# Expert gathers for 64 tokens and two ranks in place of 32 tokens and four, with the routing spread out to match

## The chip, the cores and the metric

One core of a Trainium2 chip runs the kernel, in one launch. The metric is the time of one execution in microseconds (us), measured on the device; lower is better. All arithmetic is in fp32.

## The reference, cut to what matters

One inference step of a one-layer trunk, for 1024 prompt tokens and 32 sample tokens. The change touches the last part, a retrieval feed-forward: every token has eight heads, every head picks 16 of 16384 experts, and an expert is one row of `u` and one row of `v`.

```python
def block_tail(x, o_sb, o_sw, ...):
    h = x + merged @ w_out
    return h + peer_ffn(rms_norm(h, g_ffn), w_q, keys_1, keys_2, u, v)

def peer_ffn(x, w_q, keys_1, keys_2, u, v):
    q = (xt @ w_q).reshape(t, 8, 2, 128)
    s1, s2 = q[:, :, 0] . keys_1, q[:, :, 1] . keys_2      # (t, 8, 128) each
    v1, i1 = top_k(s1, 16);  v2, i2 = top_k(s2, 16)
    best, pos = top_k(v1[..., :, None] + v2[..., None, :], 16)
    idx, gate = experts of pos, softmax(best)
    hid = gelu(einsum('thkd,td->thk', u[idx], x))
    y = einsum('thk,thkd->td', gate * hid, v[idx])
```

Ahead of it come a combined projection, stick-breaking attention over all earlier tokens, window attention with ALiBi, and the output projection. A final RMSNorm follows.

## The kernel before

**Two phases.** A projection phase (to about 350 us of the span) writes all q, k and v to scratch. The fused phase then does everything else, with every engine's program unrolled over the same line of *slots*, numbered n. Each engine walks the slots in order and issues, in a fixed order within a slot, whatever the tables `STEP_AT`, `WINDOW_AT`, `TAIL_AT`, `ROUTE_AT`, `GROUP_AT`, `X_AT` and `FINISH_AT` place there. Engines meet only through semaphores, so one that is late holds up whoever waits for it, and everything behind that wait on the waiting engine.

**The gathers.** A slot n from 0 to 1055 has one gather of 1 MB: an indirect DMA by GpSimd (L683) fetches, into each of 128 partitions, the 8 KB row `[u, v]` of one expert. Partition p belongs to one of 32 tokens and to one of four ranks (`COPIES` is 4). A group is 32 tokens and 32 gathers; a tile of 128 tokens is four groups, 128 gathers. There are eight tiles and a ninth of the 32 sample tokens: 33 groups. The ring `uv` holds seven gathers (`RING`), so gather n is issued when the expert matmuls of gather n-7 are done (`vmm`). For each gather, VectorE multiplies the u half by the tokens' x and sums (L891); for each pair of gathers (a batch) ScalarE takes gelu (L824) and makes two diagonal matrices (L830) of `gate * hid`, 128x32 each; TensorE then multiplies them with the v halves into `y_acc` (L1338). Of a batch, one gather writes one column group of 32 and the other its neighbour; the next batch writes the other two. GpSimd prepares the gates on the diagonal once in four gathers (`spread_gates`, L667).

**Once in a group.** ScalarE copies `y_acc` out (`group_out`, L840), and the first batch of the next group waits for that copy; TensorE folds the four copies together (L1326), VectorE adds (L1082). TensorE also writes x for the coming group to `o_sw` in 32 small matmuls (`copies_of_x`, L1272), and ScalarE copies it to `x_rep` in two halves (`copy_x`, L801).

**Routing.** For every head of every tile, `ROUTE_AT` places eleven stages: queries (TensorE, L1286) at offset 0, key scores at 3, seven stages of top-k on VectorE at offsets 4 to 9 and 11 (`first_eight` to `spread`), and a `select` at 10 (L1317) that brings the chosen indices into the layout of the gathers. Heads start nine slots apart, from slot 128t - 54 of tile t, and four slots apart for the first tile.

**What is placed around it.** All of it is relative to the first head's slot of a tile. `tail_slot` is 23 slots before it: merging, output projection in four quarters (L1250, slots +9 to +12), the residual on VectorE (L985, +14), its square on ScalarE (L774, +15), the turned xn (L1260, +19). `window_slot` is another 20 before that, with window attention's maximum (L934) on VectorE one slot later; it waits for a DMA of distances and window values issued two slots before. The stick-breaking steps, one in four slots, end right before the window; tile t has 2(t+1) of them, the sample tile 17.

In the running tile (positions 0 to 127 of its own slots) this places the next tile's steps up to position 29, its window at 31 to 49, its tail at 51 to 72, and its routing from 74 to position 20 of the next tile. Groups end at positions 0, 32, 64 and 96.

```python
def route_slot(t, head):
    return 4 * head - 22 if t == 0 else t * P - 54 + 9 * head
GROUP_AT = {(g + 1) * TS: g for g in range(GATHERS // TS)}
X_AT = {TS * (g - 1) + 2 * b if g else 2 * b - 18: (g, b) for g in range(GATHERS // TS) for b in range(2)}
```

## Time and profile before

| | |
|---|---|
| time, median of 3 runs | 3571.81 us (3557.09 to 3578.2) |
| time of the profiled execution | 3575.88 us |
| its span | 3574.2 us |
| VectorE busy | 63% |
| TensorE matmuls busy | 74% |
| indirect gathers | 1056, 1 MB each |
| first gather issued at | 462.83 us |

The span runs from the first to the last instruction. The shares are averages over the whole span; the fused phase has to be read by stretches. The fourth tile is cut below into eight stretches, which begin at its positions 0, 24, 40, 64, 74, 96, 104 and 112. Positions in time were found by the start of the VectorE product L891 of a given gather, which stands once per slot; the view that lists it counts two instructions for each (the product and the read of its sum).

### The profile page before, as it was taken

To read this page: it belongs to the slowest core of one execution; us is meant where nothing else is said; L and a number is where in the kernel's file an instruction comes from. 1 tells how busy PE (TensorE), PEld (TensorE's weight loads), DVE (VectorE), ACT (ScalarE), POOL (GpSimd) and SP (SyncE) were. 2 spreads that over 40 slices of the span, in tenths; PEclk is the share of its full clock that TensorE was granted. 3 is DMA by queue.
4 is the path that set the end of the run, shared out by engine and by line. 5 is a ranking of instruction groups with operands and counts; after the bars stand their busy time and mean duration, and the time that the engine had idled before them with its cause. 6 is when DMAs were issued, how large, how long until landed. Compare 5 with 4: busy or idle time off the path is not lost.

```text
span 3574.2 us, 44480 instructions
## 1 busy us (share of the span) xinstructions
PE 2648.0 (74%) x13804; PEld 1181.2 (33%) x13804; DVE 2235.2 (63%) x5671; ACT 1407.2 (39%) x3271; POOL 1434.9 (40%) x1363
## 2 busy tenths in 40 slices
PE   7998667676767777777768867887688767757675
PEld 4544342222323332333223322332244223422221
DVE  2110175578657855786568756875688557655786
ACT  1000224333632453345435633564266424443332
POOL 0000014455445534554454445444444444334543
PEclk9999687888888988898888988988999888878887
DMA  5221249999999999999899999999999999998997
GB/s 226 90 84 68 83 162 359 389 408 399 374 386 409 400 344 380 410 390 360 363 401 391 379 372 383 391 368 375 387 375 378 350 383 368 348 347 364 393 399 312
DMA packets 249016, 1210.63 MB, mean 339 GB/s; under 512 B 28944, under 2 KB 98352, under 8 KB 112592
## 3 DMA queue, kind: packets, MB, share of 16 engines
q0 software_dynamic: 156416, 1122.51, 78.8%
q1 hardware_dynamic: 92368, 85.34, 7.4%
q8 instruction: 108, 1.77, 0.2%
q14 instruction: 124, 1.02, 0.1%
HBM read 1183.96 MB, written 28.38 MB: 339 GB/s over the span
## 4 chain that ended last, share of the span: by engine, by line
PE 33%; DMA 22%; DVE 11%; issue 7%; ACTq 6%; ACT 6%; POOL 2%; DVEq 2%; SPq 0%; POOLq 0%
DMA f_uv<-peer_uv,f_idx 19%; PE f_y_acc L1338 15%; DVE f_uv L891 5%; PE f_q_ps L1286 4%; PE f_z L1250 4%; ACTq L828 3%; DMA f_work<-cache_sb_kT 3%; ACTq L716 3%; PE f_z L1143 2%; POOL f_uv L683 2%; PE f_z L1162 2%; ACT f_diag L830 2%; PE f_z L1169 1%; ACT f_work L717 1%; DMA f_work<-scratch_projT 1%
## 5 line engine op out<-in xcount | busy, mean ns | idle before, releaser
L683 POOL DMA_INDIRECT f_uv<-peer_uv,f_idx x1056 | 1247.0, 1181 | 1655.6 <-PE f_y_acc L1338 1392.3
L1338 PE MATMUL f_y_acc<-f_uv,f_diag 128*32 128x512 f32 x4224 | 1230.3, 710 | 623.1 <-ACT f_diag L830 540.2
L891 DVE CUSTOM_DVE_ANT_0 f_uv<-f_uv,f_x_rep 128x1024 f32<-128x1024 f32 x1056 | 1294.4, 1231 | 590.8 <-DMA f_uv<-peer_uv,f_idx 583.8
L1338 PEld LDWEIGHTS f_y_acc<-f_uv,f_diag 128*32 128x32 f32 x4224 | 228.0, 120 | 1279.9 <-ACT f_diag L830 719.5
L824 ACT ACTIVATE f_act_hid<-f_hid 128x2 f32<-128x2 f32 x528 | 106.8, 202 | 1070.6 <-DVE f_hid L891 1068.7
L1286 PE MATMUL f_q_ps<-w_q,f_xnT 128*128 128x256 f32 x1152 | 297.4, 416 | 28.5 <-DVE f_cut L1010 25.2
L830 ACT ACTIVATE f_diag<-f_gate_fold,f_act_hid 128x32 f32<-128x32 f32 x1056 | 282.2, 314 | 38.7 <-issue 2.8
L283 PE MATMUL proj<-xnT,w_cols 128*128 128x512 f32 (+1 forms) x864 | 283.9, 491 | 2.1 <-DVE nat L251 1.6
L1286 PEld LDWEIGHTS f_q_ps<-w_q,f_xnT 128*128 128x128 f32 x1152 | 237.2, 211 | 129.1 <-issue 56.2
L824 ACT ACT_TABLE_LOAD x207 | 265.6, 1283 | 3.8
L698 ACT ACT_TABLE_LOAD x120 | 154.0, 1283 | 254.4 <-PE f_z L1169 226.2
L667 POOL TENSOR_TENSOR f_gate_fold<-f_fold,f_gates 128x128 f32<-128x128 f32 x264 | 162.4, 615 | 125.6 <-DVE f_gates L1075 120.5
L283 PEld LDWEIGHTS proj<-xnT,w_cols 128*128 128x128 f32 x864 | 143.6, 193 | 142.8 <-issue 142.2
L241 DVE TENSOR_SCALAR stage<-proj 128x512 f32<-128x512 f32 x18 | 12.4, 692 | 270.7 <-PE proj L283 270.7
L1250 PE MATMUL f_z<-w_out_sb,f_work 128*128 128x512 f32 (+1 forms) x288 | 146.5, 664 | 25.7 <-DVE f_work L978 25.7
L304 POOL DMA_DIRECT2D scratch_projT<-stage x18 | 10.0, 555 | 311.8 <-DVE stage L241 311.8
L206 ACT ACTIVATE stage<-proj 128x512 f32<-128x512 f32 x18 | 10.8, 599 | 293.2 <-PE proj L283 293.2
L1186 PEld LDWEIGHTS f_o_sb<-f_work 128*128 128x128 f32 (+2 forms) x848 | 88.8, 169 | 55.2 <-ACT f_work L730 48.9
L1143 PE MATMUL f_z<-f_q_pad,f_work 128*128 128x256 f32 x288 | 104.9, 499 | 1.6 <-DMA f_work<-scratch_projT 1.6
L1186 PE MATMUL f_o_sb<-f_work 128*128 128x64 f32 (+2 forms) x848 | 97.8, 263 | 8.1 <-DMA f_work<-cache_sb_v 3.3
L1162 PE MATMUL f_z<-f_work,f_neg_suffix 128*128 128x512 f32 (+2 forms) x178 | 99.5, 644 | 5.3 <-DVE f_work L919 4.3
L913 DVE SCALAR_TENSOR_TENSOR f_work<-f_z,f_work 128x512 f32<-128x512 f32 (+2 forms) x89 | 56.9, 640 | 65.4 <-ACT f_work L719 61.3
(152 smaller groups left out, 2802.7 us busy)
## 6 DMA issues: line engine op xcount, KB each, us to landing
f_uv<-peer_uv,f_idx POOLq DMA_INDIRECT x1056, 9.5
f_work<-scratch_projT SPq DMA_DIRECT2D x86, 128.0 KB, 8.9
scratch_projT<-stage POOLq DMA_DIRECT2D x18, 528.0 KB, 3.9
w_cols<-w_in SPq DMA_DIRECT2D x18, 512.0 KB, 3.8
f_work<-scratch_nat SPq DMA_DIRECT2D x72, 128.0 KB
w_q<-w_peer_q SPq DMA_DIRECT2D x1, 8192.0 KB, 24.9
scratch_nat<-nat POOLq DMA_DIRECT2D x10, 512.0 KB, 3.4
x_in<-x_prompt SPq DMA_DIRECT2D x8, 512.0 KB, 4.1
```

What stands on the lines that cost most here:

```text
L283: last = nc.tensor.matmul(acc[s][:, a:b], w[:, s, k, :], xnT[:, k, a:b], start=(k == 0), stop=(k == DK - 1))
L667: nc.gpsimd.tensor_tensor(gate_fold[:, tick % 4, :, :], fold[:].unsqueeze(1).broadcast_to(full), gates[:, t % 2, head, j * PART:(j + 1) * ...
L683: pool.indirect_dma_start(uv[:, n % RING, :], None, io["peer_uv"], bass.IndirectOffsetOnAxis(ap=idx[:, t % 2, head, k:k + 1], axis=0),).th ...
L824: nc.scalar.activation(act_hid[:, tick % 2, first:first + 2], hid[:, tick % 4, first:first + 2], ACT.Gelu)
L830: made = nc.scalar.activation(diag[:, tick % 2, i, :], gate_fold[:, tick % 4, i, :], ACT.Copy, scale=act_hid[:, tick % 2, i:i + 1])
L891: nc.vector.tensor_tensor_reduce(row_u, row_u, x_rep[:, g % 2, :], 1.0, 0.0, ALU.mult, ALU.add, hid[:, tick % 4, n % PART:n % PART + 1]).t ...
L1143: last = nc.tensor.matmul(z[:, at:at + 256], kT[:, (e % 2) * 256 + m * P:(e % 2) * 256 + (m + 1) * P], q_pad[:, f, m, :, :].rearrange("p a ...
L1162: nc.tensor.matmul(out, neg_suffix[0:keys, 0:keys], sp[0:keys, 0:width], start=False, stop=False, skip_group_check=True)
L1186: last = nc.tensor.matmul(o_sb[0:n, hd * HD:(hd + 1) * HD], probs[0:keys, i * n:(i + 1) * n], v_blk[0:keys, col:col + HD], start=(e == 0 a ...
L1250: last = nc.tensor.matmul(z[0:rows, b * 512:(b + 1) * 512], mergedT[:, k, 0:rows], w_out[:, k, b * 512:(b + 1) * 512], start=(k == 0), sto ...
L1286: last = nc.tensor.matmul(q_ps[:, 0:2 * QH], xnT[:, k, :], w_q[:, k, head * 2 * QH:(head + 1) * 2 * QH], start=(k == 0), stop=(k == DK - 1))
L1338: last = nc.tensor.matmul(y_acc[i * TS:(i + 1) * TS, b * 512:(b + 1) * 512], diag[:, tick % 2, i, :], uv[:, n % RING, DM + b * 512:DM + (b ...
```

## The change

A gather now serves 64 tokens and two ranks. A group is 64 tokens and 64 gathers, so there are 17 groups, the last one of the 32 sample tokens. The diagonal matrices are 128x64, and a batch's two gathers write the two column groups of 64. `copies_of_x` has 16 matmuls where it had 32, `select` 4 where it had 16. `spread_gates` is issued after every second gather, for two ranks of 64 tokens, where it was issued before every fourth for four ranks of 32; both write 128x128. The diagonal buffer holds three batches in place of four. Routing starts 16 slots earlier in a tile and its heads are 15 slots apart (12 in the second tile, 11 in the sample tile, 8 in the first). The window, the tail and the steps, which are placed relative to it, move 16 slots earlier with it (8 slots later in the second tile). Positions in the running tile, for the third tile on: steps to 13, window 15 to 33, tail 35 to 56, routing 58 to position 46 of the next tile, groups' ends at 0 and 64.

```diff
 RING = 7
-COPIES = P // TS
+GT = 64
+COPIES = P // GT
 PART = TOPK // COPIES
+SAMPLE_COPIES = P // TS
...
-    return 4 * head - 22 if t == 0 else t * P - 54 + 9 * head
+    if t == 0:
+        return 8 * head - 22
+    return 82 + 12 * head if t == 1 else t * P - 70 + (15 if t < NT else 11) * head
...
+NG = 2 * NT + 1
...
-GROUP_AT = {(g + 1) * TS: g for g in range(GATHERS // TS)}
-X_AT = {TS * (g - 1) + 2 * b if g else 2 * b - 18: (g, b) for g in range(GATHERS // TS) for b in range(2)}
+GROUP_AT = {min((g + 1) * GT, GATHERS): g for g in range(NG)}
+X_AT = {GT * (g - 1) + 40 * (g % 2 == 0) + 2 * b if g else 2 * b - 18: (g, b) for g in range(NG) for b in range(2)}
...
-        hid = sb("hid", [P, 4, PART])
-        act_hid = sb("act_hid", [P, 2, PART])
-        gate_fold = sb("gate_fold", [P, 4, PART, TS])
-        diag = sb("diag", [P, 2, PART, TS])
+        hid = sb("hid", [P, 8, 2])
+        act_hid = sb("act_hid", [P, 4, 2])
+        gate_fold = sb("gate_fold", [P, 4, 2, GT])
+        diag = sb("diag", [P, 3, 2, GT])
...
-            hold(pool, S["routed"], 1)
-            spread_gates(0)
             for n in range(GATHERS):
                 g, t, j, head, rank = expert_of(n)
                 if rank == 0:
                     hold(pool, S["routed"], t * PH + head + 1)
-                if rank == 3 and n + 1 < GATHERS:
-                    hold(pool, S["routed"], routed_by(n // 4 + 1))
-                    spread_gates(n // 4 + 1)
                 if n >= RING:
                     hold(pool, S["vmm"], n - RING + 1)
                 k = j * PART + rank
                 pool.indirect_dma_start(uv[:, n % RING, :], None, io["peer_uv"],
                                         bass.IndirectOffsetOnAxis(ap=idx[:, t % 2, head, k:k + 1], axis=0),
                                         ).then_inc(S_UV[n % RING], 16)
+                if n % 2 == 0:
+                    spread_gates(n // 2)
...
                 for k in range(4 * b, 4 * b + 4):
                     for c in range(COPIES):
-                        last = nc.tensor.matmul(o_sw[c * TS:(c + 1) * TS, k % 4 * P:(k % 4 + 1) * P],
-                                                xnT[:, k, g % 4 * TS:(g % 4 + 1) * TS], ident[:], start=True, stop=True,
+                        last = nc.tensor.matmul(o_sw[c * GT:(c + 1) * GT, k % 4 * P:(k % 4 + 1) * P],
+                                                xnT[:, k, g % 2 * GT:(g % 2 + 1) * GT], ident[:], start=True, stop=True,
                                                 skip_group_check=True)
...
             def experts(batch):
-                tick, first = batch // 2, batch % 2 * 2
-                opens = tick % PH == 0
+                opens = 2 * batch % GT == 0
                 pe.wait_ge(S["diag"], batch + 1)
-                if opens and tick:
-                    pe.wait_ge(S["y_ev"], tick // PH)
+                if opens and batch:
+                    pe.wait_ge(S["y_ev"], 2 * batch // GT)
                 for b in range(2):
-                    for i in range(first, first + 2):
-                        n = tick * PART + i
-                        last = nc.tensor.matmul(y_acc[i * TS:(i + 1) * TS, b * 512:(b + 1) * 512], diag[:, tick % 2, i, :],
+                    for i in range(2):
+                        n = 2 * batch + i
+                        last = nc.tensor.matmul(y_acc[i * GT:(i + 1) * GT, b * 512:(b + 1) * 512], diag[:, batch % 3, i, :],
                                                 uv[:, n % RING, DM + b * 512:DM + (b + 1) * 512],
                                                 start=opens, stop=False, skip_group_check=True)
```

## Rows read from the trace of the kernel before

**Rows 1.** The page: span, busy time by engine, DMA in 40 slices.

```profile
span 3574.2 us, 44480 instructions
...
PE 2648.0 (74%) x13804; PEld 1181.2 (33%) x13804; DVE 2235.2 (63%) x5671; ACT 1407.2 (39%) x3271; POOL 1434.9 (40%) x1363
...
GB/s 226 90 84 68 83 162 359 389 408 399 374 386 409 400 344 380 410 390 360 363 401 391 379 372 383 391 368 375 387 375 378 350 383 368 348 347 364 393 399 312
```

**Rows 2.** The page's costliest groups, those of the gather and its work.

```profile
L683 POOL DMA_INDIRECT f_uv<-peer_uv,f_idx x1056 | 1247.0, 1181 | 1655.6 <-PE f_y_acc L1338 1392.3
L891 DVE CUSTOM_DVE_ANT_0 f_uv<-f_uv,f_x_rep 128x1024 f32<-128x1024 f32 x1056 | 1294.4, 1231 | 590.8 <-DMA f_uv<-peer_uv,f_idx 583.8
L667 POOL TENSOR_TENSOR f_gate_fold<-f_fold,f_gates 128x128 f32<-128x128 f32 x264 | 162.4, 615 | 125.6 <-DVE f_gates L1075 120.5
```

**Rows 3.** Stretches, L891 alone: the first 32 slots, then two whole tiles.

```profile
core 0: us, DVE busy (x), PEclk, DMA share, GB/s
494.13:601.61 107.48, 39.10 (x64) 0.77 0.73 275
...
1585.52:1957.62 372.10, 157.83 (x256) 0.86 0.96 378
...
2704.82:3099.53 394.71, 157.64 (x256) 0.86 0.94 364
```

**Rows 4.** The fourth tile in eight stretches, all engines; lengths are in the second column.

```profile
core 0: us, PE busy (x) PEld busy (x) DVE busy (x) ACT busy (x) POOL busy (x), PEclk, DMA share, GB/s
1585.52:1658.88 73.36, 62.48 (x374) 29.52 (x364) 58.11 (x151) 48.42 (x92) 31.27 (x30) 0.88 0.98 370
1658.88:1715.46 56.58, 39.94 (x204) 16.68 (x203) 26.41 (x53) 29.52 (x62) 20.21 (x22) 0.82 0.85 319
1715.46:1776.73 61.27, 41.89 (x149) 14.65 (x150) 36.94 (x73) 23.05 (x66) 28.95 (x29) 0.86 1.00 410
1776.73:1811.15 34.42, 26.58 (x154) 12.26 (x153) 16.50 (x29) 11.64 (x32) 12.88 (x13) 0.85 0.93 348
1811.15:1870.27 59.12, 41.38 (x239) 15.64 (x239) 43.85 (x120) 16.35 (x48) 33.43 (x30) 0.83 1.00 406
1870.27:1890.39 20.12, 13.78 (x116) 6.30 (x112) 18.89 (x55) 6.98 (x17) 8.08 (x8) 0.92 0.99 387
1890.39:1911.77 21.38, 16.16 (x79) 7.18 (x81) 18.98 (x54) 10.79 (x23) 10.24 (x10) 0.84 1.00 401
1911.77:1957.62 45.85, 39.51 (x210) 17.95 (x202) 40.53 (x114) 23.66 (x51) 21.52 (x20) 0.89 0.99 393
```

**Rows 5.** Who waited for whom: window attention's maximum. In total, times, longest.

```profile
DVE f_work L934 <- issue: 48.5, 7, 9.9
```

**Rows 6.** Timeline of ScalarE and VectorE at the third tile's position 65: start, length, instruction, idle.

```profile
1416.59 1.23 DVE L985 TENSOR_TENSOR f_work<-f_z,f_work 128x1024 f32<-128x1024 f32 x1 [4.44 <-PE f_z L1250]
...
1417.63 0.60 ACT L801 ACTIVATE f_x_rep<-f_o_sw 128x512 f32<-128x512 f32 x1 [11.31 <-PE f_o_sw L1272]
```

**Rows 7.** Timeline at the first gathers, GpSimd and VectorE.

```profile
462.83 1.04 POOL L683 DMA_INDIRECT f_uv<-peer_uv,f_idx  x1 [0.44 <-issue]
...
494.13 1.21 DVE L891 CUSTOM_DVE_ANT_0 f_uv<-f_uv,f_x_rep 128x1024 f32<-128x1024 f32 x1
```

**Rows 8.** Groups by line: ScalarE's diagonal and a copy of 128 columns.

```profile
L830 ACT ACTIVATE f_diag<-f_gate_fold,f_act_hid 128x32 f32<-128x32 f32 x1056 | 282.2, 314 | 38.7 <-issue 2.8
...
L794 ACT ACTIVATE f_xnT<-f_z,f_g_ffn 128x128 f32<-128x128 f32 x72 | 19.4, 376 | 3.8 <-PE f_z L1260 3.8
```

**Rows 9.** TensorE's timeline: two batches in a row, then full-width products.

```profile
700.57 1.91 PE L1338 MATMUL f_y_acc<-f_uv,f_diag 128*32 128x512 f32 x8 [0.37 <-ACT f_y_part L840]
...
703.15 1.46 PE L1338 MATMUL f_y_acc<-f_uv,f_diag 128*32 128x512 f32 x6
...
571.39 1.16 PE L1162 MATMUL f_z<-f_work,f_neg_suffix 128*128 128x512 f32 x2
...
424.62 2.31 PE L1250 MATMUL f_z<-w_out_sb,f_work 128*128 128x512 f32 x5
```

More of the change, by code:

```diff
@@ L64, in constants @@
     c["dist_sample"] = np.abs(qs[:, None] - ks[None, :]).astype(np.float32)
-    c["fold"] = np.tile(np.eye(TS, dtype=np.float32), (P // TS, 1))
+    c["fold"] = np.tile(np.eye(GT, dtype=np.float32), (P // GT, 1))
     return c
@@ L377, in fused_phase @@
         hidden = sb("hidden", [P, P])
-        fold = sb("fold", [P, TS])
+        fold = sb("fold", [P, GT])
         iota = sb("iota", [P, 2, TOPK])
@@ L482, in expert_of @@
         def expert_of(n):
-            g, s = divmod(n, TS)
-            return (g, g // 4, g % 4, *divmod(s, PART))
+            g, s = divmod(n, GT)
+            return (g, g // 2, g % 2, *divmod(s, PART if g < NG - 1 else TOPK // SAMPLE_COPIES))
         @block.sync
@@ L655, in _, with spread_gates @@
             hold(pool, S["const"], 14 * 16)
[L657 to L668 removed]
+            def spread_gates(batch):
+                g, t, j, head, rank = expert_of(2 * batch)
+                hold(pool, S["routed"], t * PH + head + 1)
+                if batch >= 4:
+                    pool.wait_ge(S["diag"], batch - 3)
+                full = [P, 2, GT]
+                k = j * PART + rank
+                nc.gpsimd.tensor_tensor(gate_fold[:, batch % 4, :, :], fold[:].unsqueeze(1).broadcast_to(full),
+                                        gates[:, t % 2, head, k:k + 2].unsqueeze(2).broadcast_to(full),
                                         ALU.mult).then_inc(S["gate_fold"], 1)
[L671 to L672 removed]
             for n in range(GATHERS):
@@ L1314, in select @@
                 sel_free(n, r)
-                for j in range(4 if t < NT else 1):
-                    for c in range(COPIES):
-                        last = nc.tensor.matmul(sel_ps[c * TS:(c + 1) * TS, j * 8:(j + 1) * 8], ident[:, j * TS:(j + 1) * TS],
-                                                packed[:, c * PART:(c + 1) * PART, :].rearrange("p k two -> p (k two)"),
+                size, copies = (GT, COPIES) if t < NT else (TS, SAMPLE_COPIES)
+                ranks = TOPK // copies
+                for j in range(rows_of(t) // size):
+                    for c in range(copies):
+                        last = nc.tensor.matmul(sel_ps[c * size:(c + 1) * size, j * 2 * ranks:(j + 1) * 2 * ranks],
+                                                ident[:, j * size:(j + 1) * size],
+                                                packed[:, c * ranks:(c + 1) * ranks, :].rearrange("p k two -> p (k two)"),
                                                 start=True, stop=True, skip_group_check=True)
@@ L1324, in fold_group @@
                 sel_free(n, sum(slot + 10 <= n for slot in ROUTE_AT))
-                rows = slice(g % 4 * TS, (g % 4 + 1) * TS)
-                nc.tensor.matmul(sel_ps[rows, :], fold[:], y_part[:, b * 512:(b + 1) * 512], start=True, stop=True,
-                                 skip_group_check=True).then_inc(S["y_fold"], 1)
+                size = GT if g < NG - 1 else TS
+                rows = slice(g % 2 * GT, g % 2 * GT + size)
+                for f in range(0, GT, size):
+                    last = nc.tensor.matmul(sel_ps[rows, :], fold[:, f:f + size], y_part[:, b * 512:(b + 1) * 512],
+                                            start=(f == 0), stop=(f + size == GT), skip_group_check=True)
+                last.then_inc(S["y_fold"], 1)
             def experts(batch):
-                tick, first = batch // 2, batch % 2 * 2
-                opens = tick % PH == 0
+                opens = 2 * batch % GT == 0
                 pe.wait_ge(S["diag"], batch + 1)
-                if opens and tick:
-                    pe.wait_ge(S["y_ev"], tick // PH)
+                if opens and batch:
+                    pe.wait_ge(S["y_ev"], 2 * batch // GT)
                 for b in range(2):
-                    for i in range(first, first + 2):
-                        n = tick * PART + i
-                        last = nc.tensor.matmul(y_acc[i * TS:(i + 1) * TS, b * 512:(b + 1) * 512], diag[:, tick % 2, i, :],
+                    for i in range(2):
+                        n = 2 * batch + i
+                        last = nc.tensor.matmul(y_acc[i * GT:(i + 1) * GT, b * 512:(b + 1) * 512], diag[:, batch % 3, i, :],
                                                 uv[:, n % RING, DM + b * 512:DM + (b + 1) * 512],
```

56 lines of the change are left out of this document (22 added, 34 removed).

## The prediction

> **What bounds the kernel now.** I read the page first. Averages name no engine as the bound: TensorE's matmuls are busy for 74% of the span and VectorE for 63% [rows 1]. The data rate does: from the eighth of the 40 slices to the last but one it stays between 344 and 410 GB/s [rows 1]. The costliest groups say who waits. Each of the 1056 gathers waits for a free buffer, and GpSimd sits idle 1392.3 us for TensorE's L1338; VectorE in turn waits 583.8 us for gathered rows [rows 2]. So work runs round a loop of seven buffers. It goes at the speed of the DMA as long as landing, product, gelu, diagonal and matmul come round in time, and at the speed of the loop where they don't.
>
> The stretches tell the two apart. Position 40 to 64 of the fourth tile takes 61.27 us for 24 slots, 2.55 us each, at 410 GB/s and a DMA share of 1.00 [rows 4]. That is the floor, and this change moves the same bytes. Against 2.55 us a slot, the eight stretches of that tile stand at +12.2, +15.8, 0, +8.9, +3.0, -0.3, +1.0 and +5.1 us [rows 4]. Their sum is 46 us of the tile's 372.10 us; the seventh tile, with the sample's long attention beside it, takes 394.71 us [rows 3]. The first 32 slots take 107.48 us, 26 over the floor [rows 3], and 31.3 us pass between the first gather's issue and the first product (462.83 to 494.13) [rows 7]. Only such excess can be won back.
>
> **The start.** Between slots -11 and 0 VectorE now works at the routing of four heads at once, about 2.9 heads' worth of stages by the offsets, so 31.3 / 2.9 = 10.8 us a head. With eight slots between heads about 1.4 remain ahead of slot 0: 15 us, unless landing takes longer. The product of slot 0 comes 16 us earlier. The first seven gathers now need one head alone where they needed two. After it, two heads less are crowded into slots 0 to 16, which I value at half of the 26 us: 13. Sum -30 us (bounds: -15, if TensorE's queries take back the second part; -42, if both parts of the excess go).
>
> **Fewer group ends.** Each of them costs ScalarE a copy, TensorE the copies of x, and the batch that opens the next group a wait. What that is worth depends on the place. At position 96, in a quiet stretch, it is nothing: 20.12 us for eight slots, -0.3 over the floor [rows 4]; I take 0.5 us. At 32 the loop is already dry, because VectorE waits there for window attention's DMA (48.5 us in 7 times [rows 5], 6.9 us each); the copy and its handshake come on top of that, 1.5 us. At 64 the end meets the tail. ScalarE stands 11.31 us at `copy_x`, since TensorE has the output projection ahead of the copies of x; gelu and diagonals of the next batch are queued behind it [rows 6]. In the new table no copy of x and no group end lies in the tail (35 to 56). The projection stays, and VectorE's 4.44 us wait for it [rows 6] too, so only what the group end adds goes: two turns of x copies and the fold, about 3 us of the 8.9. Per tile 0.5 + 1.5 + 3 = 5; eight tiles, -40 us (bounds -8 and -72, at 1 and 9 us a tile). The work saved on ScalarE, TensorE and VectorE elsewhere lies beside the DMA and counts nothing.
>
> **Routing 15 slots apart.** Position 74 to 96 prices a head on VectorE: 43.85 us busy, less 22 products at 1.24 us (1.23 in [rows 2], and its read), leaves 16.6 us for two heads, 8.3 each [rows 4]. Position 0 to 24 has 58.11 - 29.8 = 28.3 us for some 2.1 heads and six steps, so a step is about 1.8 us. Heads nine slots apart beside steps need 9 x 1.24 + 8.3 + 2.25 x 1.8 = 23.5 us in 22.95: VectorE falls behind. Fifteen apart they need 33.7 us in 38.3. The excess of the routing stretches (12.2 + 5.1 beside steps, 3.0 without) I put down to routing by half of the first and all of the second: 11.7 us a tile. In the new table about 3.6 heads lie in quiet slots at 0.8, two beside steps at 0.7, and one falls into VectorE's wait for the window's DMA, which its work fills (-1.5). But the last two now overlap window and tail, where routing never was: +2 and +1.5. That leaves about 6.5; the gain is 5 us, and I take 4. Seven tiles: -28 us. No row shows routing beside the projection, so the bounds are +21 (3 us a tile lost) and -42.
>
> **Wider operands.** A diagonal takes ScalarE about 21 ns longer (from 314 ns at 32 columns and 376 at 128 [rows 8], a third of the difference), two of them 42, and the weights load somewhat slower; where the loop sets the pace that is a seventh of some 0.1 us a batch, 5 us in all. GpSimd runs 528 gate spreads for 264, at 615 ns [rows 2]: +162 us of its time, but issued right after an even gather, when it would wait for TensorE anyway (1655.6 us idle ahead of its gathers [rows 2]). Products beside a spread are slightly longer: 3 us. Together +8 us (bounds +3, +15). If GpSimd's cover is gone, 0.6 us falls on every second gather where the loop is the bound, some 70 us.
>
> **Do the wide column groups overlap?** All else hangs on this. A batch is eight instructions of 512 columns in 1.91 us; full-width ones take 1.16 us for two and 2.31 for five, 0.38 us for each more, so eight one after the other need 1.16 + 6 x 0.38 = 3.5 us [rows 9]. The batch's two gathers thus run side by side on two column groups. The next batch does not join them: two adjacent ones take from 700.57 to 703.15 + 1.46, 4.04 us [rows 9]. The new code has two groups of 64 in a batch; I expect 1.9 us again.
>
> The Trainium skill, in TensorEngine Tiling (Array Packing), Theoretical Speedup, gives four-fold packing for 32 columns and two-fold for 64, which speaks against the change. By that page a batch would lose up to half its rate; the row at 4.04 us shows that four-fold packing was never used here.
>
> **Sum.** 3575.9 (the profiled time, 1.7 us over its span and 4 over the median of the runs) - 30 - 40 - 28 + 8 = 3486 us; less the 4 us, 3482 us.
>
> **Rivals.**
> 1. *Routing against the tail* (chance 0.2). Head seven's queries and top-k come just ahead of the projection, head six beside the window. For it: TensorE is already busy 26.58 of 34.42 us from 64 to 74 [rows 4]. Against: the queries end some six slots before the projection. Only the start and a few group ends remain: 3572 - 30 - 8 + 8 = 3542 us, and up to 3563 with the +21.
> 2. *The loop stays as it is* (0.14). The excess comes from steps, window and projection by themselves, and group ends and routing ride beside them. For it: position 24 to 40 has the largest excess with VectorE busy only 26.41 of 56.58 us [rows 4]. Then half of the start is all: 3572 - 15 + 8 = 3565 us.
> 3. *Column groups of 64 don't overlap* (0.07), the case on the other side. A batch takes 3.5 us, +1.6 for each of 64 batches a tile: 102 us more on TensorE, 281 busy us of the fourth tile's 372 [rows 4] become 383. From 0 to 24 that is 62.5 + 19 = 82 for 73 us, from 112 on 39.5 + 13 = 52.5 for 45.9; with the tail about +25 us a tile: 3482 + 8 x 25 = 3682 us. It decides once a batch takes over about 2.4 us.
> 4. *A wait replaces the old one* (0.07). The last head of the second tile is ready seven slots before its gather, and GpSimd issues about four ahead; a routing that is late by more than three slots stops the gathers. At 5 us a tile, with no gain from routing: 3482 + 28 + 40 = 3550 us; from 10 us a tile (3590) it would be slower.
> 5. *More comes back* (0.12). All bounds on the good side: 3572 - 42 - 72 - 42 + 3 = 3419 us.
>
> **How the numbers follow.** The forecast has 0.4, around 3482 us, its own range 3445 to 3530. The upper rivals reach 3565, rival 5 reaches 3419; with rival 3 left out, 3430 to 3575 holds eight in ten. A measurement of this kernel tells about 0.5% (18 us) from no change. Faster: 0.4 + rival 5's 0.12 + 0.16 of rival 1 + 0.07 of rivals 2 and 4 = 0.75. Slower: rival 3's 0.07, and 0.06 from the far ends of rivals 1, 2 and 4. Same: the remaining 0.12.
>
> **What would show it.** L1338's batch of eight at 1.9 us, its PE time as before. First product near 478 us. About 360 us for the middle tiles in place of 372; no `copy_x` wait over 3 us; L934's wait nearer 4 than 7 us; the quiet stretches still at 2.55 us a slot. Wrong if batches take over 2.4 us, if GpSimd waits for `routed` (the gates' copy) in every tile, or if the quiet slot itself changes.

## The result, and the profile after

| | median of 10 runs | lowest to highest | profiled run | its span |
|---|---|---|---|---|
| before | 3560.22 us | 3554.12 to 3578.2 | 3575.88 us | 3574.2 us |
| after | 3589.2 us | 3580.72 to 3601.93 | 3601.93 us | 3600.3 us |

The changed kernel is slower: the ratio is 1.0077 (95% interval 1.0056 to 1.0097), some 27 us. The forecast was 3482 us, with 0.75 on faster. The page of the changed kernel, to be read against [rows 1] and [rows 2]:

```profile
span 3600.3 us, 38253 instructions
...
PE 2657.9 (74%) x10640; PEld 1211.6 (34%) x10640; DVE 2225.9 (62%) x5639; ACT 1388.4 (39%) x3211; POOL 1541.9 (43%) x1627
...
L680 POOL DMA_INDIRECT f_uv<-peer_uv,f_idx x1056 | 1210.2, 1146 | 1691.4 <-PE f_y_acc L1339 1368.2
L1339 PE MATMUL f_y_acc<-f_uv,f_diag 128*64 128x512 f32 x4224 | 1300.7, 740 | 585.3 <-ACT f_diag L828 547.3
L888 DVE CUSTOM_DVE_ANT_0 f_uv<-f_uv,f_x_rep 128x1024 f32<-128x1024 f32 x1056 | 1296.6, 1235 | 598.6 <-DMA f_uv<-peer_uv,f_idx 592.8
L828 ACT ACTIVATE f_diag<-f_gate_fold,f_act_hid 128x64 f32<-128x64 f32 x1056 | 310.1, 340 | 38.0 <-issue 2.0
L669 POOL TENSOR_TENSOR f_gate_fold<-f_fold,f_gates 128x128 f32<-128x128 f32 x528 | 306.2, 580 | 10.6
```

6227 instructions fewer, among them 3164 matmuls of TensorE and as many weight loads. GpSimd is 107 us busier with its spreads, weight loads 30 us; the other engines are within 20 us of before. The loop waits as it did: GpSimd 1368.2 us for TensorE, VectorE 592.8 us for gathered rows. So the averages don't tell where 26 us of span went; the stretches do. First the start, GpSimd's first gather and VectorE's first product (compare [rows 7]):

```profile
453.02 1.01 POOL L680 DMA_INDIRECT f_uv<-peer_uv,f_idx  x1 [99.26 <-DVE f_gates L1072]
...
466.23 1.21 DVE L888 CUSTOM_DVE_ANT_0 f_uv<-f_uv,f_x_rep 128x1024 f32<-128x1024 f32 x1
```

Then the gathered part by the product's instructions alone: slots 0 to 31, 32 to 255, 256 to 895 (the third to seventh tile), 896 to 1055. After:

```profile
core 0: us, DVE busy (x), PEclk, DMA share, GB/s
466.23:552.82 86.59, 39.19 (x64) 0.88 0.94 369
552.82:1196.41 643.59, 278.27 (x448) 0.85 0.96 380
1196.41:3129.23 1932.82, 787.38 (x1280) 0.85 0.94 367
3129.23:3579.37 450.14, 198.15 (x318) 0.81 0.94 376
```

And the kernel before, in the same stretches (its first one is in [rows 3]):

```profile
601.61:1218.18 616.57, 276.67 (x448) 0.88 0.98 394
1218.18:3099.53 1881.35, 789.06 (x1280) 0.87 0.96 376
3099.53:3555.99 456.46, 196.20 (x318) 0.82 0.95 377
```

Slot 32 starts at 552.8 us instead of 601.6, 48.8 us earlier: more than the 30 forecast. Slots 32 to 255 give 27.0 us back, the five middle tiles lose 51.5 us, 10.3 each, and the last stretch gains 6.3. With 2.7 us more behind the last product the sum is the 26.1 us by which the spans differ. A second profile of the changed kernel had 1945.6 us for the middle tiles, so a difference of some 13 us over them, 2.6 a tile, says nothing.

**Where in a tile.** The fourth tile of the changed kernel, its positions 32 to 56, 56 to 64 and 64 to 80, to be read against [rows 4]:

```profile
core 0: us, PE busy (x) PEld busy (x) DVE busy (x) ACT busy (x) POOL busy (x), PEclk, DMA share, GB/s
...
1667.05:1740.63 73.58, 54.66 (x194) 21.85 (x192) 43.59 (x103) 24.93 (x66) 29.91 (x36) 0.86 0.89 345
1740.63:1762.06 21.43, 13.70 (x56) 5.79 (x54) 12.36 (x32) 5.21 (x20) 12.88 (x13) 0.92 1.02 415
1762.06:1807.56 45.50, 28.50 (x104) 10.42 (x102) 31.29 (x80) 11.90 (x32) 24.72 (x25) 0.77 0.94 378
```

The quiet stretch (56 to 64) takes 2.68 us a slot at 415 GB/s. Position 32 to 56, tail and the last head's routing, takes 3.07 us a slot with VectorE busy 43.59 and TensorE 54.66 of 73.58 us: no engine is full there, something waits.

Averaged over the third to seventh tile and laid over each other by the work they hold (a position of before is 16 later): window and the slots up to the end of the projection's matmuls (before 32 to 64, after 16 to 48) 90.4 us before, 97.8 after; the next eight slots, where VectorE waits for the projection's result, 28.2 and 27.1; all the rest of the tile, where routing and steps are, 257.7 and 261.7. That is +7.4, -1.1 and +4.0 us, the 10.3 again.

**What waits at the projection.** The changed kernel's timeline at positions 43 to 48 of the fourth tile:

```profile
1699.96 6.34 PE L1247 MATMUL f_z<-w_out_sb,f_work 128*128 128x512 f32 x8 [2.83 <-DVE f_work L975]
...
1704.76 0.23 DVE L1062 TENSOR_SCALAR f_packed<-f_gate,f_total 128x16 f32<-128x16 f32 x1
...
1706.23 1.94 PE L1339 MATMUL f_y_acc<-f_uv,f_diag 128*64 128x512 f32 x8
...
1708.10 3.70 PE L1247 MATMUL f_z<-w_out_sb,f_work 128*128 128x512 f32 x8
...
1708.94 0.97 POOL L680 DMA_INDIRECT f_uv<-peer_uv,f_idx  x1 [7.66 <-PE f_y_acc L1339]
...
1711.73 0.41 PE L1315 MATMUL f_sel_ps<-f_packed,f_ident 128*64 128x16 f32 x8
...
1712.19 0.17 DVE L1071 CAST f_idx<-f_sel_ps 128x16 uint32<-128x16 f32 x1 [4.92 <-PE f_sel_ps L1315]
...
1712.36 1.22 DVE L888 CUSTOM_DVE_ANT_0 f_uv<-f_uv,f_x_rep 128x1024 f32<-128x1024 f32 x1
...
1713.62 0.20 ACT L822 ACTIVATE f_act_hid<-f_hid 128x2 f32<-128x2 f32 x1 [6.61 <-DVE f_hid L888]
```

VectorE has packed head 7's choice at 1704.99 (`L1062`). TensorE is then in the first quarter of the output projection (6.34 us); a batch and the second quarter (3.70 us) follow before it comes to `select` (L1315) at 1711.73. VectorE stands 4.92 us for it; its next product is queued behind that wait, and ScalarE's gelu waits 6.61 us for that product. GpSimd's 7.66 us are another wait beside it: they end at 1708.94, before `select` runs, with the batch that stood behind the first quarter. The first gather of this head is ten slots further on (position 56); only the order of VectorE's queue makes the wait for `select` urgent.

The same stretch with the clock, the first quarter and then the batch and the second quarter:

```profile
core 0: us, PE busy (x) PEld busy (x) DVE busy (x) ACT busy (x) POOL busy (x), PEclk, DMA share, GB/s
1699.96:1706.23 6.27, 6.27 (x8) 2.41 (x9) 5.84 (x14) 0.36 (x3) 1.29 (x2) 0.57 1.01 421
1706.23:1711.70 5.47, 5.47 (x17) 1.92 (x16) 1.03 (x2) 0.71 (x3) 0.97 (x1) 1.00 0.48 159
```

The first quarter was slow by its clock: 0.57 granted over it, after TensorE had stood 2.83 us; at 1.00 the same eight instructions took 3.70 us. And while the loop stood, the transfers fell from 421 to 159 GB/s.

**What waits behind the group's end.** The same tile at positions 68 to 73:

```profile
1773.40 0.23 DVE L1062 TENSOR_SCALAR f_packed<-f_gate,f_total 128x16 f32<-128x16 f32 x1
...
1773.69 0.61 PE L1315 MATMUL f_sel_ps<-f_packed,f_ident 128*64 128x16 f32 x8 [1.28 <-DVE f_packed L1062]
...
1776.49 0.16 DVE L1072 COPY f_gates<-f_sel_ps 128x16 f32<-128x16 f32 x1
...
1776.75 1.08 PE L1327 MATMUL f_sel_ps<-f_y_part,f_fold 128*64 128x512 f32 x1 [2.45 <-issue]
...
1778.73 0.68 DVE L1079 TENSOR_TENSOR f_y<-f_sel_ps,f_y 64x512 f32<-64x512 f32 x1 [2.08 <-PE f_sel_ps L1327]
...
1782.10 0.97 POOL L680 DMA_INDIRECT f_uv<-peer_uv,f_idx  x1 [5.37 <-PE f_y_acc L1339]
...
1787.82 1.23 DVE L888 CUSTOM_DVE_ANT_0 f_uv<-f_uv,f_x_rep 128x1024 f32<-128x1024 f32 x1 [4.02 <-DMA f_uv<-peer_uv,f_idx]
```

Head 0's `select` and the group's fold fall in the same slot, 68, and both write `f_sel_ps`. TensorE stands 2.45 us ahead of the fold, which starts right after VectorE has read the selection (1776.49 + 0.16); then VectorE waits 2.08 us for the fold, GpSimd 5.37 us for a batch, and nine microseconds later VectorE has no gathered rows for 4.02 us.

**A third place, position 114.** VectorE's waits for `select` in the changed kernel add up to 48.6 us in 15 times. The sum by itself is no measure, since the kernel before had 58.4 us in 23; the places are. Six waits, 24.8 us, are at position 46, as above. Another 21.9 us are at position 114 of the third to seventh tile, 4.6 to 6.1 us each in the last four. In the fourth tile:

```profile
1900.40 0.23 DVE L1062 TENSOR_SCALAR f_packed<-f_gate,f_total 128x16 f32<-128x16 f32 x1
...
1901.18 3.68 PE L1339 MATMUL f_y_acc<-f_uv,f_diag 128*64 128x512 f32 x8 [3.24 <-ACT f_diag L828]
...
1904.79 2.05 PE L1140 MATMUL f_z<-f_q_pad,f_work 128*128 128x256 f32 x4
...
1906.66 1.04 PE L1159 MATMUL f_z<-f_work,f_neg_suffix 128*128 128x512 f32 x2
...
1908.49 0.41 PE L1315 MATMUL f_sel_ps<-f_packed,f_ident 128*64 128x16 f32 x8
...
1908.95 0.17 DVE L1071 CAST f_idx<-f_sel_ps 128x16 uint32<-128x16 f32 x1 [6.04 <-PE f_sel_ps L1315]
```

It is head 3, whose `select` is in slot 113. A step's scores (L1140) and another step's sums (L1159) stand in the same slot, ahead of it, behind a batch that was itself late and slow (3.68 us, granted clock 0.50).

### The profile page after: what moved, and what is told of

Read it like the earlier page. It is cut to its first block, busy times and chain, and to the rows that moved or that the text cites. A ratio compares the mean times of both kernels' runs of the same rounds, so it can differ in the third digit from the quotient of the medians.

```text
span 3600.3 us, 38253 instructions
## 1 busy us (share of the span) xinstructions
PE 2657.9 (74%) x10640; PEld 1211.6 (34%) x10640; DVE 2225.9 (62%) x5639; ACT 1388.4 (39%) x3211; POOL 1541.9 (43%) x1627
## 4 chain that ended last, share of the span: by engine, by line
PE 32%; DMA 19%; DVE 17%; issue 8%; DVEq 5%; ACT 4%; ACTq 3%; POOL 2%; SPq 1%; POOLq 0%
PE f_y_acc L1339 15%; DMA f_uv<-peer_uv,f_idx 15%; DVE f_uv L888 6%; PE f_z L1247 4%; PE f_q_ps L1282 3%; DMA f_work<-cache_sb_kT 3%; PE f_z L1140 2%; ACTq L826 2%; PE f_z L1159 2%; POOL f_uv L680 1%; ACTq L715 1%; DVEq L1040 1%; PE f_z L1166 1%; DVEq L1053 1%; ACT f_diag L828 1%
## 5 line engine op out<-in xcount | busy, mean ns | idle before, releaser
L680 POOL DMA_INDIRECT f_uv<-peer_uv,f_idx x1056 | 1210.2, 1146 | 1691.4 <-PE f_y_acc L1339 1368.2
L1339 PE MATMUL f_y_acc<-f_uv,f_diag 128*64 128x512 f32 x4224 | 1300.7, 740 | 585.3 <-ACT f_diag L828 547.3
L888 DVE CUSTOM_DVE_ANT_0 f_uv<-f_uv,f_x_rep 128x1024 f32<-128x1024 f32 x1056 | 1296.6, 1235 | 598.6 <-DMA f_uv<-peer_uv,f_idx 592.8
L1339 PEld LDWEIGHTS f_y_acc<-f_uv,f_diag 128*64 128x64 f32 x4224 | 312.5, 159 | 1237.9 <-ACT f_diag L828 710.0
L828 ACT ACTIVATE f_diag<-f_gate_fold,f_act_hid 128x64 f32<-128x64 f32 x1056 | 310.1, 340 | 38.0 <-issue 2.0
L669 POOL TENSOR_TENSOR f_gate_fold<-f_fold,f_gates 128x128 f32<-128x128 f32 x528 | 306.2, 580 | 10.6
L1282 PE MATMUL f_q_ps<-w_q,f_xnT 128*128 128x256 f32 x1152 | 273.6, 392 | 4.6 <-ACT f_xnT L793 2.3
L1282 PEld LDWEIGHTS f_q_ps<-w_q,f_xnT 128*128 128x128 f32 x1152 | 220.1, 195 | 75.5 <-issue 35.6
L1315 PE MATMUL f_sel_ps<-f_packed,f_ident 128*64 128x16 f32 (+1 forms) x576 | 33.5, 232 | 114.0 <-DVE f_packed L1062 107.8
L1140 PE MATMUL f_z<-f_q_pad,f_work 128*128 128x256 f32 x288 | 105.8, 502 | 1.1 <-DMA f_work<-scratch_projT 1.1
```

The source lines that it names most:

```text
L669: nc.gpsimd.tensor_tensor(gate_fold[:, batch % 4, :, :], fold[:].unsqueeze(1).broadcast_to(full), gates[:, t % 2, head, k:k + 2].unsqueeze ...
L680: pool.indirect_dma_start(uv[:, n % RING, :], None, io["peer_uv"], bass.IndirectOffsetOnAxis(ap=idx[:, t % 2, head, k:k + 1], axis=0),).th ...
L828: made = nc.scalar.activation(diag[:, batch % 3, i, :], gate_fold[:, batch % 4, i, :], ACT.Copy, scale=act_hid[:, batch % 4, i:i + 1])
L888: nc.vector.tensor_tensor_reduce(row_u, row_u, x_rep[:, g % 2, :], 1.0, 0.0, ALU.mult, ALU.add, hid[:, n // 2 % 8, n % 2:n % 2 + 1]).then_ ...
L1140: last = nc.tensor.matmul(z[:, at:at + 256], kT[:, (e % 2) * 256 + m * P:(e % 2) * 256 + (m + 1) * P], q_pad[:, f, m, :, :].rearrange("p a ...
L1282: last = nc.tensor.matmul(q_ps[:, 0:2 * QH], xnT[:, k, :], w_q[:, k, head * 2 * QH:(head + 1) * 2 * QH], start=(k == 0), stop=(k == DK - 1))
```

## The experiments

Each run's ratio is to the kernel before on the same chip, with its 95% interval. Before's medians there were 3571.31 to 3573.14 us, so ratios are what is compared. By the intervals, a difference of two ratios is uncertain by some 0.003 to 0.004, 11 to 13 us. All edits are on the changed kernel.

**1. The groups alone, with the whole old table.**

```diff
-    if t == 0:
-        return 8 * head - 22
-    return 82 + 12 * head if t == 1 else t * P - 70 + (15 if t < NT else 11) * head
+    return 4 * head - 22 if t == 0 else t * P - 54 + 9 * head
```

> The group of 64 alone: both parts of the table are those of before (4 slots apart in the first tile, 9 in the others). By my prediction's terms (group ends -40 us, wider operands +8 us, part of the start) it is at 0.99 or below. If a group end is worth nothing, as the tiles of e1_table_9 say, the ratio is 0.998 to 1.004.

3577.48 us, ratio 1.0006 (0.9979 to 1.0032). Half as many group ends, half the copies of x, 4 matmuls for a `select` in place of 16, and wide diagonals together come to nothing that can be measured (-8 to +11 us by the interval). The middle tiles took 1895.0 us, before 1881.35. Position 64 to 80 of a tile took 50.4 us, before 49.9. The 11 us at `copy_x` [rows 6] is gone and its place is taken in part: ScalarE waits 51.7 us in 12 times for the last batch before it can copy `y_acc` out, in eight of them 4.9 to 6.1 us at position 66, right behind the projection.

**2. Only the start, eight slots apart; later tiles by the old table.**

```diff
-    if t == 0:
-        return 8 * head - 22
-    return 82 + 12 * head if t == 1 else t * P - 70 + (15 if t < NT else 11) * head
+    return 8 * head - 22 if t == 0 else t * P - 54 + 9 * head
```

> Groups of 64 as changed, but the routing table of before from the second tile on (first head at 128t - 54, heads nine slots apart); the first tile keeps eight slots. Nothing else differs. Theory A (the new places of the routing cost the time: heads six and seven beside window and tail, heads beside the group's end): the middle tiles go back from 376-400 us to 353-375 us or a little less, the start stays 49 us shorter than before; about 3515 us, ratio to before 0.985 to 0.99. Theory B (the group of 64 itself costs it: wider weights, twice the gate spreads, fewer small matmuls and a lower TensorE clock): the middle tiles stay near 376-400 us and the time near 3590 us, ratio about 1.007.

3540.4 us, ratio 0.9905 (0.988 to 0.993). Slot 32 starts at 556.2 us, in experiment 1 at 599.0; slots 32 to 255 take 640.7 us, there 627.3. Of 42.8 us won, 13.4 come back; that is about half of what it lies over the 3515 us expected. Its middle tiles stand with those of the kernel before:

```profile
556.22:1196.93 640.71, 278.27 (x448) 0.85 0.96 379
1196.93:3075.59 1878.66, 796.35 (x1280) 0.87 0.96 376
```

**3. The changed kernel without the spread-out start** (`4 * head - 22` in the first tile).

> The changed kernel with the heads of the first tile four slots apart, as before, in place of eight. If the shorter start comes from that spacing, most of the 49 us gained up to the product of slot 32 are lost again: about 3625 us. If it comes from the group alone (seven gathers that need one head), the start keeps over half of it: below 3605 us.

3619.49 us, ratio 1.014 (1.0109 to 1.017): the start is worth 23 to 30 us here too (0.0063 to 0.0084), and all else that the change does costs more than it gains.

**4. The changed kernel again**, beside later ones.

> The changed kernel itself again, as the reference for the other runs of this chip. Every theory: ratio to before 1.004 to 1.010.

3591.68 us, ratio 1.0056 (1.0032 to 1.0079).

Experiments 1, 2 and 4 split the change by ratio: groups of 64 +0.0006 (2 us), the start -0.0101 (-36 us), the new table of the later tiles +0.0151 to +0.0172 (54 to 61 us). It was the table with the routing 15 slots apart, forecast at -28, that made the kernel slower.

**5. Twelve apart in place of 15**, third to eighth tile.

```diff
-    return 82 + 12 * head if t == 1 else t * P - 70 + (15 if t < NT else 11) * head
+    return 82 + 12 * head if t == 1 else t * P - 70 + (12 if t < NT else 11) * head
```

> The changed kernel with heads 12 slots apart in place of 15 from the third to the eighth tile, first head at 128t - 70 as changed. The last head starts at position 14 in place of 35, so no routing lies beside the output projection, and its last stages end at 25. Theory A: positions 32 to 63 go back to the floor, five of the ten us a tile: six tiles, about 3555 us. Theory B: no change beyond 5 us.

3553.39 us, ratio 0.9945 (0.9926 to 0.9964). The middle tiles take 1892.8 us, 40 less. Where: positions 16 to 48, with the window and heads 6 and 7, took 97.8 us a tile and now take 89.6. No `select` meets the projection or a step's slot any longer: VectorE's wait for L1315 falls from 48.6 us to 1.1. The steps' stretch (80 to 128) hardly moves as a whole, 146.6 to 145.4 us, though its heads are closer; within it, 104 to 128, where head 3's `select` had waited, takes 6.0 us less a tile and 80 to 104 takes 4.8 more.

**6. Half of the gate spreads narrow** (2 columns wide; the batches concerned use the gates of earlier ones).

```diff
-                full = [P, 2, GT]
+                wide = GT if batch % 2 == 0 or batch < 4 else 2
+                full = [P, 2, wide]
```

> The changed kernel in which every second gate spread writes 2 columns of 64 instead of all (from the fifth batch on), so that those batches use gates of an earlier one; GpSimd's spreads cost about what they did before. If the doubled spreads cost time (theory B in part), it gets faster by up to 20 us; by my prediction by 3 us or less.

3583.96 us, ratio 1.0031 (1.0012 to 1.005), against 1.0056 and 1.0077. Its interval overlaps that of experiment 4, not the first one; the extra 144 us of GpSimd's spreads are worth 9 to 16 us at most by these, where I had 3, and perhaps nothing.

**7. The last head five slots earlier** (position 30 in place of 35, its `select` at 40, ahead of the projection at 44).

```diff
-    return 82 + 12 * head if t == 1 else t * P - 70 + (15 if t < NT else 11) * head
+    if t == 1:
+        return 82 + 12 * head
+    return t * P - 70 + (15 * head - 5 * (head == 7) if t < NT else 11 * head)
```

> The changed kernel with the last head of the third to eighth tile five slots earlier (position 30 in place of 35), so that its select is in slot 40, before the output projection begins in slot 44; in the changed kernel the select stands behind two quarters of it, and VectorE waits some 5 us at position 46. Theory A3 (that select behind the projection is what head seven costs): most of the 5 us a tile at positions 32 to 47 go, 20 to 30 us in all. Rival A4 (what costs is eight slots of routing on VectorE between window and tail, wherever they are): within 8 us, either way.

3568.81 us, ratio 0.9988 (0.996 to 1.0016), 0.0068 or 24 us under experiment 4: one head, whose `select` no longer stands behind the projection. Positions 32 to 56 go from 73.6 us to 69.6 in its profile, and none of VectorE's waits for `select` is left at position 46; those at 114 stay. The middle tiles:

```profile
1192.03:3105.73 1913.70, 790.92 (x1280) 0.85 0.95 371
```

**8. Fold and add of a group two slots later** (70 and 71, 74 and 75).

```diff
-                    if (g := GROUP_AT.get(n - 5 - 4 * b)) is not None:
+                    if (g := GROUP_AT.get(n - 7 - 4 * b)) is not None:
                         add(g, b)
...
-                added = sum(slot + 4 + 4 * b < n for slot in GROUP_AT for b in range(2))
+                added = sum(slot + 6 + 4 * b < n for slot in GROUP_AT for b in range(2))
...
-                    if (g := GROUP_AT.get(n - 4 - 4 * b)) is not None:
+                    if (g := GROUP_AT.get(n - 6 - 4 * b)) is not None:
                         fold_group(g, b, n)
```

> The changed kernel with the fold and the add of a group two slots later (offsets 6 and 10, 7 and 11 in place of 4 and 8, 5 and 9). In the changed table head 0 has its select in slot 68, the slot of the fold of the group that ends at 64, and the fold must wait until VectorE has read the select. Theory A1 (this meeting costs time: TensorE waits for VectorE, VectorE for TensorE): positions 64 to 80 lose 3 us of their excess in each of seven tiles, VectorE's add waits no longer; 15 to 25 us faster than the changed kernel. Rival A2 (the meeting is harmless, all of the loss is heads six and seven beside window and projection): within 5 us of the changed kernel.

3581.21 us, ratio 1.0034 (1.0014 to 1.0055); 8 us under experiment 4, with overlapping intervals, so by the time it stands between the two theories. The place itself is clear: positions 64 to 80 take 42.7 us a tile, with the fold at 68 45.8. At the other group end the wait comes up anew, VectorE 5.0 to 6.1 us for the fold at position 7; positions 0 to 32 are no longer for it in sum (98.4 us, 98.7).

**9. Heads 14 apart and the later fold together.** If meetings are the cause, they should add up.

```diff
-    return 82 + 12 * head if t == 1 else t * P - 70 + (15 if t < NT else 11) * head
+    return 82 + 12 * head if t == 1 else t * P - 70 + (14 if t < NT else 11) * head
...
```

The other edits are those of experiment 8.

> The changed kernel with two edits at once: heads of the third to eighth tile 14 slots apart instead of 15 (heads 6 and 7 at positions 14 and 28 instead of 20 and 35, so that the last select comes at 38, ahead of the projection at 44), and the group's fold and add two slots later (70 and 74 instead of 68 and 72), off the select of head 0. Theory: the loss of the middle tiles is made of three meetings of routing with something else: select behind the projection (24 us in the run with that head alone moved), fold and select in one slot (about 9 us), and head 6 beside the window (up to 25 us in the run 12 apart, here perhaps a third to a half of that, 8 to 12). Their sum, 41 to 45 us off the 3590 us of the changed kernel: 3545 to 3550 us, a ratio near 0.993 to the kernel before, and about 1888 to 1895 us for slots 256 to 895. Rival: it is how far apart the heads are spread that costs, evenly in slots: then one third of the way from 15 to 12 gives a third of 37 us, and the later fold at most 9: 3569 us, ratio 0.999, some 1910 us for these slots.

3549.72 us, ratio 0.9948 (0.9923 to 0.9973). The sum came out nearly: 0.0108 under experiment 4, 39 us for 41 to 45, against a rival that gave 3569. The loss of the middle tiles is gone, and of VectorE's waits for `select` 2.7 us are left:

```profile
1195.12:3074.61 1879.49, 793.99 (x1280) 0.87 0.96 377
```

```profile
DVE f_idx L1071 <- PE f_sel_ps L1315: 2.7, 4, 1.3
```

The places don't all agree with my accounting, though. In us for the stretches of a tile, mean of the third to seventh:

| positions | before | after | 12 apart | head 7 early | fold later | 14 and fold |
|---|---|---|---|---|---|---|
| 0 to 32 | 99.4 | 98.7 | 94.3 | 98.2 | 98.4 | 98.7 |
| 32 to 56 | 68.9 | 73.6 | 69.4 | 69.6 | 73.8 | 71.7 |
| 56 to 64 | 21.5 | 21.8 | 21.8 | 22.1 | 21.6 | 21.7 |
| 64 to 80 | 49.9 | 45.8 | 47.8 | 45.4 | 42.7 | 42.1 |
| 80 to 104 | 64.3 | 65.3 | 70.1 | 66.0 | 66.9 | 67.8 |
| 104 to 128 | 72.3 | 81.3 | 75.3 | 81.4 | 80.0 | 73.9 |

(The column of before holds other work at these positions; only its sum, 376.3, compares.) The fold's 3.7 us are where they should be, and half of head 7's 4.0. But positions 0 to 32, where head 6 beside the window was to give 8 to 12 us in all, gave nothing; 4.9 us a tile came from 80 to 128, where the middle heads are. So the fold's share is shown, head 7's by experiment 7 and here by half, and the third is wrong in place. What I had left out is position 114: 14 apart, head 3's `select` is in slot 110, where no step stands, VectorE's wait of up to 6.1 us is gone, and 104 to 128 takes 7.4 us less a tile (in experiment 5, where that wait is gone too, 6.0 less). Both runs give 2.5 to 4.8 us of it back at 80 to 104, and no run moved head 3 alone, so what this meeting costs in all isn't shown.

**10. Window and tail clear of routing and of group ends, heads nine apart.** First tile as in the changed kernel; window 12 to 30, tail 32 to 53, routing 55 to 1, group ends 0 and 64.

```diff
-    return 82 + 12 * head if t == 1 else t * P - 70 + (15 if t < NT else 11) * head
+    return (74 if t == 1 else t * P - 73) + 9 * head
```

> Groups of 64, first tile eight slots apart, then heads nine slots apart from 128t - 73 (second tile 128 + 74 - 128 = 74): the routing ends at position 1, nothing of it lies beside window (12 to 30) or tail (32 to 53), no group end and no copy of x lies in the tail, and no select meets a fold. Beside e1_table_9 it differs from the third tile on in that alone: there the tail (51 to 72) holds the group end at 64. If a group end in the tail costs what I predicted (3 us a tile), it is 15 to 25 us faster than e1_table_9 (ratio to before about 0.985). If the tail's excess is the projection's own, it is within 5 us of it (about 0.990).

3617.61 us, ratio 1.0141 (1.0098 to 1.0184): as slow as experiment 3, with the tidiest table, and outside both theories (0.985 and 0.990). Its middle tiles took 1952.9 us.

**11. The same, one slot earlier** (`t * P - 74` in place of `t * P - 73`, from the third tile on).

> As e8_all_clear, but the table one slot earlier (first head at 128t - 74, the second tile unchanged), so that the attention steps stand in odd slots again, as in before, the changed kernel and e1, and window, tail and routing stay clear of each other. In e8 the steps stood in even slots. Theory P (the parity of the steps to the batches, which TensorE and ScalarE take in odd slots, sets what a step costs): the steps' stretch falls back to the 21.4 us a slot-column of before, 25 to 40 us less than e8 a tile's steps allowing, and the clear window and tail remain: about 3525 us, ratio 0.985 to 0.99, not above e1_table_9. Theory Q (the early place itself, e.g. the copies of x at position 104 among the steps, costs the time): within 10 us of e8, ratio about 1.012.

3530.29 us, ratio 0.9877 (0.9845 to 0.9909), the lowest ratio here. One slot is worth 0.0264 of the time, 94 us (some 19 either way). Its four stretches:

```profile
468.74:558.61 89.87, 39.32 (x64) 0.89 0.94 361
558.61:1187.68 629.07, 278.79 (x448) 0.88 0.97 387
1187.68:3077.26 1889.58, 793.30 (x1280) 0.88 0.96 376
3077.26:3504.64 427.38, 198.13 (x318) 0.82 0.99 397
```

**12. Experiment 2 with its table one slot earlier** (`t * P - 55` for `t * P - 54`, so that steps stand in even slots).

> e1_table_9 with the whole table from the second tile on moved by one slot (first head at 128t - 55 in place of 128t - 54), nothing else. Theory P: the steps stand in even slots, and the ratio to before goes from 0.990 to 1.01 or more. Theory Q: within 0.3% of e1_table_9.

3579.41 us, ratio 1.0022 (0.9996 to 1.0049), against 0.9905: 42 us lost, between the two theories (1.01 or more; within 0.003). The two profiled executions differ by less, 11 us, as this one was among the quicker of its kernel and that of experiment 2 its slowest. By their stretches, the shift wins 27.2 us in slots 32 to 255 (613.5 us for 640.7) and 14 behind 896, and loses 52.6 between: the middle tiles take 1931.3 us for 1878.7, more than all of it at positions 0 to 32, where the steps are (118.3 us a tile for 98.5); the stretch from 32 to 56 is even 9.7 us shorter. Gelu and the expert matmuls are issued in odd slots. In the faster tables the steps stand in odd slots too, and ScalarE's two stages of a step, one and five slots later, in even ones; shifted by one, they stand in the odd slots, in the queue ahead of gelu. ScalarE's wait for the sums of a step, in experiment 2 and then in this one (total, times, longest):

```profile
ACT L695 <- PE f_z L1164: 233.3, 62, 7.4
```

```profile
ACT L695 <- PE f_z L1164: 310.6, 58, 10.7
```

77 us more in fewer waits shows which queue is disturbed, not by which meeting; the order ahead of gelu is a candidate that no run isolates.

## Why the prediction was wrong

**The step that failed: routing 15 slots apart, -28 us.** The term, the whole new table of the later tiles, measured +54 to +61 us, outside its own bounds of -42 and +21. I read the excess of the routing stretches as VectorE falling behind (23.5 us of work in 22.95) and so took distance for the cure. No stretch shows that gain: as laid over each other above, the one with routing and steps went from 257.7 to 261.7 us with heads nearly twice as far apart, and even in experiment 9, without the waits for `select`, it is 254.9, 2.8 us less, which is hardly more than two profiles of one kernel differ by. Busy time near the length of a stretch was at most a small part of what bound it. What 15 apart did do was put single matmuls of the routing into slots where an engine's in-order queue holds longer work ahead of them: `select` behind the projection cost 24 us (experiment 7), the fold on head 0's `select` some 8 (experiment 8), head 3's `select` behind a step an amount that no run separates, and going back to 12 apart won 0.0111 to 0.0132, 40 to 47 us, in all.

**Rival 1 had the place, not the mechanism or the size.** It named head 7 just ahead of the projection, and I argued against it that "the queries end some six slots before the projection". That looked at the stages at offsets 0 to 3 and not at the one at offset 10: `select` comes at 45, inside the projection's 44 to 47. The stages of a moved head have to be followed to the last of its matmuls. Its bound of +3 us a tile was less than half of the 8 measured (54 to 61 us over seven tiles), since it priced overlap by busy time where the price was a wait: 4.92 us on VectorE with gelu behind it.

**Fewer group ends, -40 us: nothing.** Groups alone gave 1.0006 with their wider operands, so ends and widths together are +2 us where I had -32. I took VectorE's and ScalarE's waits at position 65 for the group end's. With only the group end there and no x copies (experiment 1) positions 56 to 72 take 49.9 us a tile, and with neither of them (experiment 11, the same work at 36 to 52) 49.5; before it was 49.7. There the projection was last in the wait all along, and `copy_x` only stood in line behind it. Experiment 10, also with neither, took 45.6 us for the same work one slot later, so the place isn't fixed by the projection alone; a group end of its own cost shows in none of them. `copy_x` indeed no longer waits over 3 us (13.1 us in 9 times, longest 2.5), which the prediction named as its proof and which proved nothing about time. The wait at the window did not shrink either: 40.1 us in 6 times, 6.7 each, where I had 4. That it is a wait for the DMA was my reading; the row [rows 5] names no releaser. Rival 2 ("the loop stays as it is") was right on this half.

**The start, -30 us: right as a sum, wrong in its parts.** The first product came 28 us earlier, not 16 (466.2 us for 494.1), and slot 32 48.8 us earlier; then 13 of it were lost again by slot 255 (experiment 2 against 1). Why is open: the first tile's last heads, which now stand at slots up to 45, explain little, as slots 32 to 48 take only 1.8 us more, while 8.7 are lost in slots 128 to 192, where the two tables are the same; and in experiment 12, with the same start, slots 32 to 255 are 13.8 us shorter than in experiment 1. Net 23 to 36 us by the ratios of experiments 1 to 4.

**Wider operands, +8 us:** not separated from zero. A diagonal took 340 ns for 314 (I had 21 ns more; it is 26). The batch was as forecast:

```profile
701.80 1.94 PE L1339 MATMUL f_y_acc<-f_uv,f_diag 128*64 128x512 f32 x8
```

1.94 us for 1.91 [rows 9]: two column groups of 64 run side by side, and rival 3 is out. One after the other the eight would need 3.5 us [rows 9]. The Trainium skill, in TensorEngine Tiling (Array Packing), Theoretical Speedup, gives up to two-fold for 64 columns, and this row agrees with it. The up to four-fold that it gives for 32 columns did not show in the kernel before [rows 9], where two batches took 4.04 us, so nothing was lost. The mean of all 4224 was 740 ns for 710, and the mean granted clock of the span 0.854 for 0.868. Which of the two follows from the other wasn't tried.

**Rival 4** (routed late) didn't come up: besides the first gather's 99.3 us, GpSimd waited 3.1 us for `routed`. **Rival 5** needed the two terms that failed.

With each term at its measured value, -36 for the start, +2 for groups and widths and +54 to +61 for the table, the sum is +20 to +27 us. That it meets the measured +20 (experiment 4) and +27 is no proof, since the three are differences along one row of kernels and must add up to it. The one independent value is the start's in experiment 3, -23 to -30, so some 6 to 13 us hang on what the start is combined with, or on noise.

**What stays open.** Why one slot of parity costs 42 and 94 us: the steps' stretch and ScalarE's waits show where, but no run moved steps alone against the batches, and in experiment 12 the early tiles gained by the same shift. What heads 3 and 6 cost, each alone: 12 apart gave time back beside the window and behind position 104, 14 apart only there. And why experiment 11 is the fastest: its interval overlaps that of experiment 2, its gain over it lies in slots 32 to 255 (629.1 for 640.7) and behind 896 (427.4 for 456.6), while its middle tiles are 11 us longer, which is within what two profiles of one kernel differ by (13 us).

## What to carry to other kernels

Where each engine walks a fixed order of slots, list every slot of every stage that a table moves, the last as well as the first, and look what long work the same engine has in that slot; 0.41 us of TensorE's work, queued behind a batch and a quarter of the projection, stopped VectorE for 4.92 us here, and ScalarE's gelu behind it. Read a wait by what would end it last if the named work were gone, before counting that work's removal as a gain. And when a table is shifted, try it one slot to either side: here one slot was worth 94 us, about the 90 forecast for the whole change.

## What the runs showed that I had not expected

- Parity: two tables that differ by one slot in where steps, window, tail and routing stand took 3617.61 and 3530.29 us (experiments 10 and 11), and 3579.41 and 3540.4 us (12 and 2).
- Removing 6215 of 44480 instructions, net, TensorE's matmuls and weight loads above all, without a change of the order around the loop left the time as it was: 1.0006 (0.9979 to 1.0032), experiment 1.
- The spread of gates on GpSimd took 0.41 us at 1700.87 and 1.13 us at 1775.59 of the changed kernel's profile (0.41 to 1.48 us over all, median 0.41), and the issue of a gather 0.93 to 2.04 us (median 0.97). What sets it wasn't tried.
